# A two-layer decoder trunk on one core: layer 0's second swish moved out of the last weight block, shorter orders at the joints, and heads scored in pairs

## The reference, cut to what matters

```python
def even_mixer(h, w_in, w_out):
    aq, ak, av, rq, rk, rv, rg = jnp.split(h @ w_in, [s1, s2, s3, s4, s5, s6], axis=-1)
    a_out = moba_attention(rotary(split_heads(aq, 8)), rotary(split_heads(ak, 8)), split_heads(av, 8))
    r_out = retention(retnet_rotation(split_heads(rq, 4)), retnet_rotation(split_heads(rk, 4)), split_heads(rv, 4))
    r_out = merge_heads(r_out) * jax.nn.silu(rg)
    return jnp.concatenate([merge_heads(a_out), r_out], axis=-1) @ w_out
...
    for layer in range(DEPTH):
        h = h + mixer(rms_norm(h, mix_norm), w_in, w_out)     # even_mixer, then odd_mixer
        h = h + hier_moe(rms_norm(h, ffn_norm[layer]), ...)   # top group of 4, top 2 of its 8 experts
    return rms_norm(h, final_norm)
```

## Time and profile before

| | |
|---|---|
| median of 3 runs | 1150.01 us (1148.75 to 1153.74) |
| time of the profiled execution | 1149.47 us |
| its span, first to last instruction | 1147.6 us |
| TensorE matmul busy | 868.9 us (76%) |
| VectorE busy | 393.9 us (34%) |
| ScalarE busy | 237.3 us (21%) |
| read from HBM | 439.53 MB, 384 GB/s over the span |
| mean granted TensorE clock | 0.888 of full |

### The profile page before, as it was taken

The page is one execution under the profiler, slowest core; times in us unless marked ns, Lnnn a source line. Parts: engine busy times, 40 slices in busy tenths (PEclk is TensorE's granted clock), DMA queues, the critical chain, the costliest instruction groups (busy, mean ns, idle before and its releaser), DMA issues.

```text
span 1147.6 us, 21805 instructions
## 1 busy us (share of the span) xinstructions
PE 868.9 (76%) x9162; PEld 550.9 (48%) x9162; DVE 393.9 (34%) x990; ACT 237.3 (21%) x618; POOL 29.0 (3%) x47
## 2 busy tenths in 40 slices
PE   8988979967575757576799999798666666675774
PEld 6865745534242434343478776355343434343432
DVE  5886632412121212121178764233121212121212
ACT  5555411100000000000065762011000000000002
POOL 0002000000000000000000220000000000000000
PEclk9998989988787888888999999899787979788888
DMA  9865699999999999999996576999999999999995
GB/s 341 259 296 224 260 400 415 428 428 427 429 429 427 428 429 429 428 429 427 419 387 259 217 309 253 415 425 429 429 429 429 429 427 428 428 428 428 429 428 219
DMA packets 54270, 441.22 MB, mean 384 GB/s; under 512 B 11856, under 2 KB 12368, under 8 KB 29648
## 3 DMA queue, kind: packets, MB, share of 16 engines
q1 hardware_dynamic: 54080, 440.07, 92.3%
q10 hardware_dynamic: 144, 0.52, 0.1%
HBM read 439.53 MB, written 1.05 MB: 384 GB/s over the span
## 4 chain that ended last, share of the span: by engine, by line
DMA 43%; PE 40%; DVE 5%; SPq 4%; ACT 3%; another core or an unknown queue 3%; issue 2%; POOLq 0%; POOL 0%; ACTq 0%; DVEq 0%
DMA ring<-in_w_expert_up 21%; DMA ring<-in_w_expert_down 21%; PE bank L994 11%; PE bank L1013 5%; PE bank L888 3%; PE bank L890 3%; PE bank L889 3%; PE bank L976 3%; PE bank L1026 2%; SPq L438 2%; PE bank L1062 1%; PE bank L1064 1%; PE bank L1063 1%; SPq L439 1%
## 5 line engine op out<-in xcount | busy, mean ns | idle before, releaser
L994 PE MATMUL bank<-ring,scratch 128*32 128x256 f32 x4096 | 301.9, 460 | 179.2 <-DMA ring<-in_w_expert_up 177.7
L994 PEld LDWEIGHTS bank<-ring,scratch 128*32 128x32 f32 x4096 | 156.7, 132 | 319.8 <-issue 208.2
L1450 DVE TENSOR_SCALAR scratch<-scratch 128x128 f32<-128x128 f32 x64 | 14.6, 228 | 633.4 <-ACT scratch L688 611.6
L687 ACT ACTIVATE scratch<-bank 128x128 f32<-128x128 f32 x64 | 17.7, 277 | 601.5 <-PE bank L994 582.8
L1013 PE MATMUL bank<-ring,h 128*32 128x256 f32 x2048 | 127.2, 390 | 12.0 <-DMA ring<-in_w_expert_down 12.0
L1026 PE MATMUL bank<-h 32*128 32x256 f32 x1024 | 74.3, 402 | 37.2 <-ACT h L695 37.2
L1013 PEld LDWEIGHTS bank<-ring,h 128*32 128x32 f32 x2048 | 63.6, 111 | 56.1 <-issue 25.4
L1026 PEld LDWEIGHTS bank<-h 32*128 32x128 f32 x1024 | 50.0, 186 | 67.0 <-issue 66.9
L888 PE MATMUL bank<-split,h_high 128*128 128x512 f32 x192 | 77.6, 404 | 6.0 <-DVE split L1250 6.0
L1250 DVE SCALAR_TENSOR_TENSOR split<-ring,gains,split 128x512 fp32r<-128x512 f32 x96 | 68.0, 749 | 23.6 <-ACT split L730 22.9
L890 PE MATMUL bank<-split,h_high 128*128 128x512 f32 x192 | 75.0, 391 | 0.0
(11 more groups left out here) (179 smaller groups left out, 754.6 us busy)
## 6 DMA issues: line engine op xcount, KB each, us to landing
ring<-in_w_expert_gate SPq DMA_DIRECT2D x64, 2048.0 KB, 47.4
ring<-in_w_expert_up SPq DMA_DIRECT2D x64, 2048.0 KB, 48.9
ring<-in_w_expert_down SPq DMA_DIRECT2D x64, 2048.0 KB, 48.6
ring<-in_w_in_even SPq DMA_DIRECT2D x5, 2048.0 KB, 17.8
ring<-in_w_in_odd SPq DMA_DIRECT2D x5, 2048.0 KB, 20.4
ring<-in_w_out_even SPq DMA_DIRECT2D x2, 2048.0 KB, 9.6
ring<-in_w_out_odd SPq DMA_DIRECT2D x2, 2048.0 KB, 12.1
h<-in_x SPq DMA_DIRECT2D x2, 512.0 KB, 4.7
```

Source lines behind the costliest of these rows:

```text
L994: last = pe.matmul(psum[6][32 * j:32 * j + 32, 0:2 * P].rearrange("p (a s) -> p a s", a=2), xT[:, c, SLOTS * k:SLOTS * k + SLOTS], ring[:, ...
```

## The change

Six edits, all in the orders of the engines and what goes with them.

- In layer 0 the second swish leaves block 5: its first half stands behind the last decay, its second half behind the maximum of head 1. The scores of retention heads 2 and 3 and the first two decays move into block 5. The four `retain` stand together, behind the scores of the first two heads. The product of the router's weights with their gains moves behind the last head.
- Layer 0's heads are scored two at a time on two row tiles of TensorE, as layer 1's were.
- The squares and the root chain of a layer's first block move behind chunks 4 and 5.
- The last quarter of h that is turned for the router is copied by ScalarE, not VectorE. The places come ahead of the counting of the rounds (`count_rounds`), and the counts go to another PSUM bank. Behind the assignment there is one warm-up product where there were three.
- The last down block of a layer is loaded in two halves, and its products wait for each half. At the end of layer 0 one warm-up product and not three stands around the turns, and VectorE copies the sums back ahead of the first two low parts.
- The final gain row is loaded once (4 KB) and spread to all partitions by TensorE (a product with ones) and ScalarE.

```diff
@@ block.sync
+            def load_last_down(l, free):
+                sp.wait_ge(down_done[l], free + 1)
+                for half, arrived in enumerate((down_arrived[l][GE - 1], down_rest)):
+                    cols = slice(2 * D * half, 2 * D * half + 2 * D)
+                    sp.dma_start(ring[:, DOWN_AT[GE - 1], cols], down_rows[(l + 1) * EXPERTS - 1][:, cols])\
+                      .then_inc(arrived, 16)
...
-                for e in range(EXPERTS - 6, EXPERTS - GE):
-                    next_down(l, more * EXPERTS + e, e + GE, e % GE)
+                next_down(l, more * EXPERTS + EXPERTS - 6, EXPERTS - 2, GE - 2)
+                load_last_down(l, more * EXPERTS + EXPERTS - 5)
@@ block.scalar
-                    if last and l == LAYERS - 1 and k == 0:
+                    spreading = last and l == LAYERS - 1 and k < T
+                    if spreading and k == 0:
                         act.wait_ge(gate_up_done[l], e + 1)
-                        act.dma_start(gain_row, final_norm.partition_broadcast(P)).then_inc(fin_loaded, 16)
+                        act.dma_start(gain_row[0:1, :], final_norm.partition_broadcast(1)).then_inc(fin_loaded, 16)
                     finish_expert(l, e)
+                    if spreading:
+                        act.wait_ge(gain_spread, k + 1)
+                        act.copy(gain_rows[:, 512 * k:512 * k + 512], psum[5][:, :]).then_inc(gain_copied, 1)
...
                     parts(4, COPY_AT[0])
+                    if j == 0:
...
...
                     square(2 * l + 1, t, 1)
-                    if t == 0:
-                        turned_out(0, 1)
+                    turned_out(t, 1)
@@ block.tensor
                 if m >= 2:
-                    pe.wait_ge(s_out[l], m - 1 if l == 0 else m - 2)
+                    pe.wait_ge(s_out[l], m if l == 0 else m - 2)
                 elif l == 0:
-                    pe.wait_ge(ret_ready, RET - 1 + m)
-                heads = [(score_bank(l, n), slice(HEAD * (n % 2), HEAD * (n % 2) + HEAD))
-                         for n in ((m,) if l == 0 else (m, m + 1))]
+                    pe.wait_ge(ret_ready, RET)
+                heads = [(score_bank(l, n), slice(HEAD * (n % 2), HEAD * (n % 2) + HEAD)) for n in (m, m + 1)]
...
+            def spread_gains(half):
+
+                if half:
+                    pe.wait_ge(gain_copied, half)
+                else:
+                    pe.wait_ge(fin_loaded, 16)
+                keep_warm(2, cst[:, 0:512], psum[5])
+                pe.matmul(psum[5][:, :], const("ones")[0:1, :], gain_row[0:1, 512 * half:512 * half + 512],
+                          start=True, stop=True).then_inc(gain_spread, 1)
...
+                    if l == 0 and j == NW - 1:
+                        for i in range(2, RET):
+                            item_scores(l, i)
                     project(l, j, TURN_AT[1], C)
-                for i in range(n_items[l] + LAG + 3):
+                for i in range(begun_items[l], n_items[l] + LAG + 3):
...
-                    if 0 <= i - 2 < n_ret[l]:
-                        retain(i - 2)
+                        for n in range(n_ret[l]):
+                            retain(n)
...
-                keep_warm(2, cst[:, 0:512], psum[0])
+                pe.matmul(psum[7][:, 0:32], ones, asg[:, 0, :], start=True, stop=False)
+                keep_warm(1, cst[:, 0:512], psum[0])
                 pe.wait_ge(assigned, T * l + 2)
-                pe.matmul(psum[4][:, 0:32], ones, asg[:, 1, :], start=False, stop=True).then_inc(counts_done, 1)
+                pe.matmul(psum[7][:, 0:32], ones, asg[:, 1, :], start=False, stop=True)
                 pe.matmul(psum[6][:, 32:64], before, asg[:, 1, :], start=False, stop=True).then_inc(pos_done, 1)
-                keep_warm(1, cst[:, 0:512], psum[0])
...
-                    keep_warm(2, cst[:, 0:512], psum[5])
+                    keep_warm(1, cst[:, 0:512], psum[5])
                     for q in range(2):
...
-                    keep_warm(1, cst[:, 0:512], psum[3])
@@ block.vector
                     if 0 < j <= ROTATED[l]:
                         rotate(l, T * (j - 1) + 1, link)
-                    if swishing:
-                        swish(j - RG - 1, 1, link)
+                    if l == 0 and j == RG + 1:
+                        swish(0, 1, link)
+                    if l == 0 and j == NW - 1:
+                        dve.wait_ge(const_loaded[2], 3 * 16)
+                        for n in range(2):
+                            decayed(n)
...
                 if l == 0:
+                    for n in range(2, RET):
+                        decayed(n)
+                    swish(1, 0, link)
...
                     if m < HEADS[l]:
                         head_max(l, m)
+                    if l == 0 and m == 1:
+                        swish(1, 1, link)
...
                 places(l, route_link)
 
                 choose_slots(l, 0, 0)
+                count_rounds(l, route_link)
                 columns(l, 0)
...
-                if l < LAYERS - 1:
-                    dve.wait_ge(gain_loaded[2 * l + 2], 16)
-                    split_chunks(l + 1, 0, 0, AHEAD)
                 dve.wait_ge(scattered[l], (more + 1) * EXPERTS)
                 if l < LAYERS - 1:
                     for q in (1, 3):
                         dve.tensor_copy(h[:, :, QUARTER * q:QUARTER * q + QUARTER], acc[q]).then_inc(h_odd_back, 1)
+                    dve.wait_ge(gain_loaded[2 * l + 2], 16)
+                    split_chunks(l + 1, 0, 0, AHEAD)
```

98 lines of the change are left out of this document (47 added, 51 removed).

## The result

The changed kernel takes 1143.52 us (median of 7 executions, 1142.95 to 1145.78); the kernel before, run beside it, 1152.72 us (1148.75 to 1153.74). The ratio is 0.9938, 95% interval 0.9925 to 0.9951: faster by 0.6%, just beyond the 0.5% at which a measurement tells a change from none. The profiled execution took 1143.52 us, its span 1141.7 us; that is 6.0 us less than the profiled execution of before, where 7.0 were forecast. Between the medians of the runs shown here it is 9.2 us, by the ratio, which goes by all of them, about 7.1.

What follows compares the result with a forecast made beforehand. The weight stream bounds most of the span; only time in which it rests can be won. Terms 3.2 - 0.2 + 1.9 - 0.2 + 2.1 = 6.8, say 7, off 1149.5 give 1142.5 us; range 1137 to 1149.

Steps and rivals of the forecast that it cites:

- Squares, layer 0: First block of layer 0: squares and root chain behind chunks 4 and 5 shorten TensorE's wait, gaining 0.6 us.
- Block 5 and the heads: Layer 0: without the second swish block 5 ends 2.3 us sooner; head 2's maximum comes 5.3 us sooner, head 7's 5.2.
- The second rival: Layer 0's head stage: the swish is only moved and paid back there; 1 us of 4.6 stays, 1146.1 us; chance 0.26.
- Pairs of heads: Layer 0's heads: a pair costs TensorE no more than one head; retention steps cover the new 0.95 us wait.
- The clock in heads and mixing: Layer 0: sparser TensorE work lowers the clock early, back only within the mixing; cost 2.0 us, between 0 and 3.4.
- The third rival: Layer 0's mixing: the fallen clock is not granted back; 1154.4 us if all 33 us run low; chance 0.06.
- Routing: Last mixed product to gate and up: 1.0 us gained, 1.2 lost to the clock; net -0.2 a layer, +1.0 to -2.4.
- My own sign of a wrong prediction: Gather in both layers: running at half clock throughout was one of three signs that would make the prediction wrong.
- The joint: Layer 0's last down block to layer 1's chunk 6: net 1.9 us gained, between 0.6 and 2.3, after 0.4 for the clock.
- The end: Layer 1's end: 4 KB gain row saves 1.2 us of stream, halved down block 0.95; together 2.1, between 0.9 and 2.2.
- The first rival: Whole kernel: the clock costs nothing, so 11.6 us are gained, giving 1137.9 us; chance 0.20.
- my case: Whole kernel: the main forecast, 1142.5 us with clock costs counted, own range 1139.5 to 1145.5 us; chance 0.48.

Runs made afterwards that it cites:

- experiment 12: Kernel of experiment 9 with the squares and root chain of both layers' first blocks ahead of chunk 4 again; 1141.50 us, ratio 0.9916.
- experiment 1: Changed kernel with both halves of layer 0's second swish back in block 5; 1147.12 us, ratio 0.9968.
- experiment 2: Changed kernel with layer 0's heads scored one at a time again, the four retain still together; 1143.92 us, ratio 0.9939.
- experiment 8: Changed kernel with two warm-up products added at each of two places between layer 0's heads; 1142.90 us, ratio 0.9928.
- experiment 6: Changed kernel with layer 0's old end order (three warm-up products around the turns, low parts before VectorE's copies), down block still halved; 1143.94 us, one execution.
- experiment 7: Kernel of experiment 4 with each layer's last down block loaded whole; 1144.70 us, one execution.
- experiment 5: Changed kernel with the squares and root chain of each layer's first block ahead of chunk 4 again; 1144.62 us, one execution.
- experiment 10: Changed kernel without any edit, run again on the chip of experiment 9; 1144.39 us, ratio 0.9948.
- experiment 4: Changed kernel with four more warm-up products ahead of layer 1's last pair of weights; 1143.64 us, ratio 0.9937.
- experiment 9: Changed kernel with warm-up products added between layer 0's heads, at both gathers (three, not one) and ahead of the last pair (four); 1140.05 us, ratio 0.9909.

## Why the prediction came out right, step by step

The predicted 1142.5 us is 1.0 us below the measured median, and the sum of 7.0 stands against 6.0 of the two profiled executions. The terms were less good than the sum, and part of its closeness is luck: two came out 2.5 us short together, two others 1.5 us over.

- **Squares, layer 0: 0.6 expected.** 0.56 at chunk 6 (experiment 12). Right.
- **Block 5 and the heads: head 2 5.3 us sooner expected, head 7 5.2.** 5.59 and 5.60. Right, and through the mechanism named: the swish went into VectorE's waits, and undoing it alone costs 3.1 us (experiment 1). The 0.3 to 0.4 us more fit the `retain` lump, 2.92 us and not 3.5; that was not tried by itself. The second rival, the swish only moved and paid back in the heads, is out.
- **Pairs of heads: no cost, no gain.** So it is (experiment 2); the expected cover held.
- **The clock in heads and mixing: 2.0 taken, bounds 0 and 3.4.** Between head 7 and the last add the kernel lost 1.55 us, which experiment 8 gave back in full; in other executions it was up to 2.6, so 2.0 was well sized. The last add came 4.05 us sooner, 3.2 expected. I expected one long low stretch into the mixing; there were two, with a full clock between, and only the second, 3.5 us long, reached the mixing, for its first 1.2 us. The third rival, no clock in the mixing, did not come near.
- **Routing: 1.0 gained, 1.2 lost a layer.** The gain is 1.30 us in layer 0 (5.35 - 4.05) and 1.04 in layer 1. These gains are read from distances alone; no run undoes the earlier places or ScalarE's copy. The loss is 1.61 and 2.06 us, all in the gather. This term was sized too low: I took a value near the low end because before the clock came back within 3.5 us of falling. What matters is not how long it is low but what it lies on, and the two warm-up products removed were what it had lain on. Net -0.3 and -1.0, where -0.2 was expected. My own sign of a wrong prediction, "if the gather runs at half clock throughout in both layers", did not come true as written: the clock was at half up to 146.0 us of a gather that ran from 142.67 to 148.09, and up to 706.0 of one that ran from 701.50 to 707.37. But the low clock met it in both layers, and in every other trace with one warm-up product.
- **The joint: 1.9 net, 0.4 of it set aside for the clock.** From the end of the last down block to chunk 6 it is 1.35 us less (0.87 for the orders, 0.5 for the squares, by experiments 6 and 12), and by experiment 7 the halves are worth 1.0: 2.35, with the clock full. Against the kernel before, though, it is less: from the start of layer 0's last gate and up to chunk 6 it is 27.01 us before and 25.29 now, 1.72. The down block's share of that is 0.37 us (11.77 and 11.40 to its end): before, the block's product began 9.84 us behind the pair, here the second half landed only 10.33 us behind it. What delays it here is not known.
- **The end: 2.1, between 0.9 and 2.2.** This is the step that failed, and its range failed with it. The halved block is worth 0.76 us, and between TensorE's waits for the weights of expert 29 and of expert 31, with the row's transfer between them, it is 29.36 us in the changed kernel (1087.79 to 1117.15), 29.36 or 29.37 in experiments 5, 6, 8 and 10, and 30.64 before (1092.99 to 1123.63): 1.28 us, which I put down to the row's 508 KB; no run tests it by itself. That much was as forecast. But from the last pair on the changed kernel lost 0.65 us, because gate and up ran at half clock and took 2.5 us more. I had put a clock term into three places and none here, although the row that I quoted shows TensorE idle for 3.21 us ahead of the pair before this one, and that pair took 5.35 us in all, with the clock at half from 1109.5 to 1113 us. I read the row as room for the spreading and not as a sign of the clock. Two warm-up products and the spreading end sooner than the four products that stood there, and the wait ahead of the last pair grew from 1.83 to 3.17 us. With the clock kept the end is worth what was forecast (experiment 4). Measured from the first gate and up of layer 1: 0.58 us.

Against the sum of 6.8, the end came out 1.5 us short and the two gathers 0.9; layer 0's heads and mixing brought 0.85 more, and the stretch from the first gate and up to layer 1's last add 2.54 us in place of 1.9. That makes 5.83 us, what the final norm's first product shows; the rest of the 6.0 lies behind it. Of the 2.54, 1.02 us were won inside layer 0's expert loop, between the first gate and up and the last (4.76 us ahead there), and belong to none of my terms. The loop's third gate and up took 4.71 us before (175.53 us, half clock to 177.5) and 3.66 now (170.91), and when TensorE next waits for weights the lead is 4.85 us (239.18 and 234.33): a low stretch cost before and not now. No run tests this. The first rival, 1137.9 us without any cost of the clock, is what experiment 9 moves towards (1140.05): the mechanism that separated my case from it was the right one.

**The clock, by rule and by row.** The prediction weighed the rule of the Trainium skill, page TensorE: Matmul & The Clock Gate, Part 1, that the low clock is the default and only sustained activity lifts it; by it the cost in the heads was 3.4 us. The trace showed 1.55 us more than before, and 2.6 at the most in any trace. The same part of that page of the Trainium skill says that how many products of one kernel run slow differs from run to run; the two profiles of the changed kernel agree with that (5.42 and 5.15 us for the first gather's 32 products).

## What to carry to other kernels

When an edit takes idle or filler work off an engine with a throttled clock, ask which instruction a low stretch will now lie on: a filler product in a gap is cheap, since it takes the slow time in place of the work behind it. Put it in every gap that ends in work on the critical path, the last wait for weights above all, and let it run until that work can begin: the four products that ended 2.5 us ahead of layer 0's last pair kept its clock full in six traces of 14 only. Size the edits with the clock kept, then without. Before a step is read off two traces by its time, look whether both stood at the same place ahead of it: here one and the same code stood up to 2.1 us apart (block 5's first scores, 74.96 to 77.03 us). A transfer that is moved from "needed at the end" to "needed by the next step" must be looked at for its latency within a full stream, not for its bytes.

## What the runs showed of the hardware that was not expected

- The clock falls at moments that differ between executions of one program (91.5 and 101.5 us, then 92.0 and 102.5; 142.5, then 140.0), and in two executions of 14 profiled (experiments 5 and 10) it stood at half right at the start of the projection (about 10.3 to 13.7 us and 10.1 to 13.5 us). Ahead of it TensorE had waited 2.33 us in experiment 10 and 1.97 us in the first profile of the same program, where the clock stayed full.
- A stretch of little work does not always lower the clock: in experiment 12 it was full from 134 to 147 us, with 3.1 us of warm-up products in it, while in experiment 9, with the same products, it was at half from 136.5 to 140 us.
- A 4 KB load on ScalarE's queue landed within 4.7 to 5.2 us beside the full weight stream (12 traces), 512 KB in 11.1 to 11.2 us, about nine times the 1.2 us that its bytes take at 428 GB/s.
- Four `retain` in a row, 24 products, took 2.92 us, where one between two scores took 0.91 us for its six.
